# Strassen-Winograd for three weight blocks: seven half-size products in place of eight in layer 0's in-projection

## The reference

```python
for l in range(2):
    h = rms_norm(x, norm_mix[l])
    x = x + mixer_l(h)            # one input projection, two kinds of heads, one output projection
    h = rms_norm(x, norm_ffn[l])
    x = x + hierarchical_moe(h)   # 32 experts, top-1 group, top-2 inside it
```

```python
rq, rk, rv, rg, hq, hf, hi, hg = split(h @ w_in, 8)
ret = rms_norm(retention(rope(rq), rope(rk), rv)) * silu(rg)
o   = rms_norm(hgrn2(silu(hq), 1 - f(hf), hi, log f(hf))) * silu(hg)
return concat([ret, o]) @ w_out
```

## Time and profile before

| | us |
|---|---|
| median of 3 runs | 1168.29 (1167.1 to 1169.87) |
| the profiled execution | 1165.02 |
| its span in the trace | 1163.2 |
| TensorE busy in the span | 883.9 (76%) |
| VectorE busy in the span | 221.5 (19%) |
| ScalarE busy in the span | 130.3 (11%) |
| DMA read | 445.61 MB from HBM |

### The profile page before, as it was taken

How to read it: one execution, slowest core, us unless ns; L and a number is a source line. 1 busy time by engine, 2 the same in 40 slices (tenths; PEclk the granted TensorE clock), 3 DMA queues, 4 the chain that set the end, 5 groups by cost and what they waited for, 6 DMA issues and landing times.

```text
span 1163.2 us, 11675 instructions
## 1 busy us (share of the span) xinstructions
PE 883.9 (76%) x5180; PEld 404.4 (35%) x5180; DVE 221.5 (19%) x478; ACT 130.3 (11%) x271; POOL 0.5 (0%) x5
## 2 busy tenths in 40 slices
PE   9999999947474747475899999996474747474768
PEld 7555545412121212121346655443131313131313
DVE  2732332100000000000127541411010101010101
ACT  3411311000000000000021431200000000000000
POOL 0000000000000000000000000000000000000000
PEclk9999999968787878787999999998787878787889
DMA  9776769999999999999996577799999999999996
GB/s 348 303 297 274 280 221 374 434 433 433 433 438 433 436 433 433 431 431 416 425 422 286 181 292 294 306 438 433 433 438 435 432 433 429 433 431 433 421 425 284
DMA packets 20215, 447.49 MB, mean 385 GB/s; under 512 B 2624, under 2 KB 2880, under 8 KB 5824
## 3 DMA queue, kind: packets, MB, share of 16 engines
q1 hardware_dynamic: 20160, 446.67, 91.3%
HBM read 445.61 MB, written 1.05 MB: 384 GB/s over the span
## 4 chain that ended last, share of the span: by engine, by line
DMA 51%; PE 45%; DVE 1%; another core or an unknown queue 1%; issue 1%; ACT 1%; SPq 0%; DVEq 0%
DMA places<-in_together 43%; PE psum L692 16%; PE psum L1100 11%; PE psum L1212 5%; DMA places<-in_singles 4%; DMA places<-in_quarters 4%; PE psum L1097 4%; PE psum L610 1%; PE psum L1113 1%; PE psum L1141 1%; PE psum L593 1%; PE psum L586 0%; DMA places<-in_w_in 0%; PE psum L757 0%
## 5 line engine op out<-in xcount | busy, mean ns | idle before, releaser
L692 PE MATMUL psum<-places,mixed 128*32 128x512 f32 x3040 | 420.0, 703 | 266.5 <-DMA places<-in_together 239.3
L692 PEld LDWEIGHTS psum<-places,mixed 128*32 128x32 f32 x3040 | 110.0, 127 | 553.6 <-issue 445.1
L1100 PE MATMUL psum<-places 128*128 128x512 f32 x288 | 126.3, 593 | 0.0
L1100 PEld LDWEIGHTS psum<-places 128*128 128x128 f32 x288 | 53.6, 190 | 61.4 <-issue 61.2
L610 PEld LDWEIGHTS psum<-sel,x 128*128 128x128 f32 x528 | 60.8, 192 | 16.6 <-issue 16.0
L610 PE MATMUL psum<-sel,x 128*128 128x128 f32 x528 | 64.6, 279 | 0.3
L593 PE MATMUL psum<-y_sb,spread 128*128 128x512 f32 x128 | 59.6, 606 | 2.1 <-ACT y_sb L844 1.4
L892 DVE SCALAR_TENSOR_TENSOR sig<-psum,slot_scale,sig 128x512 f32<-128x512 f32 x16 | 12.0, 750 | 238.3 <-ACT sig L835 238.3
L895 DVE SCALAR_TENSOR_TENSOR mixed<-psum,slot_scale,sig 128x512 f32<-128x512 f32 x16 | 12.0, 751 | 230.0 <-PE psum L692 230.0
L905 DVE COPY y_sb<-psum 128x512 f32<-128x512 f32 x14 | 9.7, 691 | 192.4 <-PE psum L692 192.4
L837 ACT COPY mixed<-psum 128x512 f32<-128x512 f32 x16 | 9.4, 586 | 323.7 <-PE psum L617 323.7
(11 more groups left out here) (259 smaller groups left out, 524.8 us busy)
## 6 DMA issues: line engine op xcount, KB each, us to landing
places<-in_singles SPq DMA_DIRECT2D x28, 2048.0 KB, 11.6
places<-in_quarters SPq DMA_DIRECT2D x22, 2048.0 KB, 35.8
places<-in_w_in SPq DMA_DIRECT2D x12, 2048.0 KB, 26.7
places<-in_w_out SPq DMA_DIRECT2D x4, 2048.0 KB, 14.0
places<-in_singles SPq DMA_DIRECT2D x4, 1024.0 KB, 5.2
places<-in_quarters SPq DMA_DIRECT2D x4, 1024.0 KB, 46.5
places<-in_singles SPq DMA_DIRECT2D x2, 1280.0 KB, 6.1
places<-in_w_in SPq DMA_DIRECT2D x2, 1024.0 KB, 26.8
```

Of the source, the lines that this page charges most:

```text
L692: mm = pe.matmul(psum[slots, out + n, :], inp[:, c, slots], slot(layer, unit)[:, at + 512 * n:at + 512 * (n + 1)], start=c == 0, stop=c == ...
L1100: mm = pe.matmul(banks[:, m, :], hT[:, c, m * P:(m + 1) * P], w[:, c, :], start=c == 0, stop=c == KC - 1)
```

## The change

For units 5, 6 and 7 (`SEVEN`), the 256x1024 by 1024x512 product is cut in two along each dimension: A into A11, A12, A21, A22 (token half, width half; each 128x512), B into B11, B12, B21, B22 (each 512x256), the result into four corners c11, c12, c21, c22 of 128x256. `project_seven` computes seven products of such blocks, each by 4 matmuls of 128x128 by 128x256, instead of the eight that the plain product has. VectorE makes the sums of blocks (`sides_of_seven` once, `first_sums`, `second_sum` and the last line of `add_fourth_product` for each unit, in part in place in the weights) and joins the products (`keep_first_product` to `add_corner`). The four side blocks and two weight sums lie in place 9, so the DMA of expert unit 9 moves in SP's order from behind `roped` 2 to behind unit 1. VectorE's order is rewritten, with `gated_norm` cut into `norm_asked`, `refine_root`, `norm_out` and `norm_gained` among the joins; ScalarE's waits for these units are for `summed` (5 for each unit) in place of the unit's end.

```diff
+SEVEN = (5, 6, 7)
...
-                    sp.wait_ge(S["roped"], 2)
-                    load_expert_unit(0, 9)
                     load_expert_unit(0, 3)
...
                     load_expert_unit(0, 1)
+                    load_expert_unit(0, 9)
                     sp.wait_ge(S["gated"], 2)
...
+            def project_seven(n, meanwhile=()):
+                k = SEVEN.index(n)
...
+                def product(dst, left, right, opens):
+                    for c in range(4):
+                        mm = pe.matmul(dst, left[:, c, :], right[:, c, :], start=opens and c == 0, stop=c == 3,
+                                       skip_group_check=True)
+                    return mm
+                product(c11, hT[:, 0:4, 0:P], w[:, 0:4, 0:256], True).then_inc(S["product"], 1)
+                pe.wait_ge(S["sums_ready"], 2 * k + 1)
+                product(c22, side_2, sum_b, True).then_inc(S["product"], 1)
+                pe.wait_ge(S["summed"], 5 * k + 1)
+                product(c12, side_1, sum_a, False).then_inc(S["product"], 1)
+                pe.wait_ge(S["summed"], 5 * k + 2)
+                product(c21, side_3, w[:, 0:4, 256:512], False).then_inc(S["product"], 1)
+                for step in meanwhile:
+                    step()
+                pe.wait_ge(S["summed"], 5 * k + 3)
+                product(c11, hT[:, 4:8, 0:P], w[:, 4:8, 0:256], False)
+                product(c12, side_4, w[:, 4:8, 256:512], False).then_inc(S["product"], 1)
+                pe.wait_ge(S["summed"], 5 * k + 4)
+                pe.wait_ge(S["sums_ready"], 2 * k + 2)
+                product(c21, hT[:, 4:8, P:SEQ], w[:, 0:4, 0:256], False).then_inc(S["unit_used"], 1)
...
-            project(0, 5)
+            project_seven(5)
...
-            project(0, 6)
+            project_seven(6)
...
-            project(0, 7, {8: (lambda: turn_half(0, 0),)})
+            project_seven(7, (lambda: turn_half(0, 0),))
...
+            def sides_of_seven():
+                a11, a12, a21, a22 = hT[:, 0:4, 0:P], hT[:, 4:8, 0:P], hT[:, 0:4, P:SEQ], hT[:, 4:8, P:SEQ]
+                turn(V.tensor_tensor(side_1, a21, a22, ALU.add))
+                turn(V.tensor_tensor(side_2, side_1, a11, ALU.subtract))
+                turn(V.tensor_tensor(side_3, a11, a21, ALU.subtract))
+                turn(V.tensor_tensor(side_4, a12, side_2, ALU.subtract))
...
+            def first_sums(k):
+                b11, b12, b21, b22 = blocks_of(k)
+                wait_unit(dve, 0, SEVEN[k])
+                if k > 0:
+                    dve.wait_ge(S["product"], 5 * k - 2)
+                turn(V.tensor_tensor(sum_a, b12, b11, ALU.subtract))
+                turn(V.tensor_tensor(sum_b, b22, sum_a, ALU.subtract))
+            def second_sum(k):
+                b11, b12, b21, b22 = blocks_of(k)
+                V.tensor_tensor(b12, b22, b12, ALU.subtract).then_inc(S["sums_ready"], 1)
+            def keep_first_product(k):
+                dve.wait_ge(S["product"], 5 * k + 1)
+                and_wait(dve, V.tensor_copy(corner, corners(SEVEN[k])[0]), S["summed"], 5 * k + 1)
...
+            def add_fourth_product(k):
+                c11, c12, c21, c22 = corners(SEVEN[k])
+                b11, b12, b21, b22 = blocks_of(k)
+                dve.wait_ge(S["product"], 5 * k + 4)
+                V.tensor_tensor(c22, with_c12, c21, ALU.add).then_inc(S["summed"], 1)
+                V.tensor_tensor(b11, b21, sum_b, ALU.subtract).then_inc(S["sums_ready"], 1)
+            def add_corner(k):
+                c11, c12, c21, c22 = corners(SEVEN[k])
+                dve.wait_ge(S["product"], 5 * k + 5)
+                V.tensor_tensor(c12, c12, corner, ALU.add)
+                wait_projected(dve, SEVEN[k] + 1)
+                V.tensor_tensor(c21, c21, corner, ALU.add).then_inc(S["summed"], 1)
...
             rope_ret(3, GROUP_W)
+            sides_of_seven()
+            first_sums(0)
+            second_sum(0)
             mask(1, st2[:, 1, :], const("causal_scale"))
+            keep_first_product(0)
+            add_second_product(0)
+            add_third_product(0)
+            add_fourth_product(0)
+            first_sums(1)
+            second_sum(1)
+            add_corner(0)
             mask(2, st2[:, 2, :], const("causal_scale"))
...
+            norm_asked(0)
             mask(7, st2[:, 3, :], const("causal_scale"))
+            keep_first_product(1)
+            refine_root(dve, turn)
+            add_second_product(1)
+            norm_out(0, 6, 0)
+            add_third_product(1)
+            norm_gained(0, 0)
+            add_fourth_product(1)
+            first_sums(2)
+            add_corner(1)
+            second_sum(2)
+            silu_gate(6, gates_in[0])
+            gate_it(0, gates_in[0], 0)
+            keep_first_product(2)
+            norm_asked(1)
+            add_second_product(2)
+            refine_root(dve, turn)
+            add_third_product(2)
+            norm_out(1, 4, GROUP_W)
+            add_fourth_product(2)
+            norm_gained(1, GROUP_W)
+            add_corner(2)
+            silu_gate(7, gates_in[1])
+            gate_it(1, gates_in[1], GROUP_W)
```

More of the change, by code:

```diff
@@ L207, in build @@
         sin_t, cos_t = rope[:, 0], rope[:, 1]
+        at_nine = wide[:, (9 - RING) * UNIT:(10 - RING) * UNIT]
+        sum_a, sum_b = [at_nine[:, 1024 * i:1024 * (i + 1)].rearrange("p (c n) -> p c n", c=4) for i in range(2)]
+        side_1, side_2, side_3, side_4 = [at_nine[:, 512 * i:512 * (i + 1)].rearrange("p (c t) -> p c t", c=4) for i in range(4, 8)]
         val = part(0, 10, 1024, "p (c n) -> p c n", c=TC)
@@ L233, in build @@
         spread = sb("spread", [P, TC, P])[:, :, :]
+        corner, with_c12 = flat_pair(spread), flat_pair(sel)
         sig = sb("sig", [P, FF])[:, :]
@@ L267, in build @@
         names = ["small_landed", "tables_landed", "in_half_landed", "begin_landed", "begin_second", "begin_third", "begin_fourth", "gains_landed", "xt_first_landed", "xt_second_landed", "xt_third_landed", "even_dims", "odd_dims", "gather_begun", "xT_begun", "half_landed", "x_first_landed", "x_second_landed", "first_landed", "pos_landed", "lb_landed", "router_landed", "masks0_landed", "masks_landed", "consts_landed", "filler_ready", "unit_used", "stored",
-                 "act_turn", "dve_turn", "rope_args", "rope_ready", "pos_ready",
+                 "act_turn", "dve_turn", "product", "sums_ready", "summed", "rope_args", "rope_ready", "pos_ready",
                  "squares", "x_start_turned", "hT_first", "hT_second", "diag_ready", "row_done", "f_scaled", "q_scaled", "lb_in", "lb_exp",
@@ L355, in proj, with corners @@
             return psum[:, 2 * (g % 2):2 * (g % 2) + 2, :]
+        def corners(n):
+            banks = proj(n)
+            return [banks[:, tc, 256 * h:256 * (h + 1)] for tc in range(2) for h in range(2)]
         def wait_projected(eng, n):
@@ L1104, in project @@
                 mm.then_inc(S["unit_used"], 1)
+            def project_seven(n, meanwhile=()):
+                k = SEVEN.index(n)
+                wait_unit(pe, 0, n)
+                pe.wait_ge(proj_used[n % 2], n // 2)
+                w = slot(0, n).rearrange("p (c n) -> p c n", c=KC)
+                c11, c12, c21, c22 = corners(n)
+                def product(dst, left, right, opens):
[18 more added lines that the diff above has]
+                product(c21, hT[:, 4:8, P:SEQ], w[:, 0:4, 0:256], False).then_inc(S["unit_used"], 1)
             def project_first():
@@ L1475, in keep_values @@
             def keep_values(dst, g, ready):
-                wait_projected(act, g + 1)
+                if g in SEVEN:
+                    act.wait_ge(S["summed"], 5 * SEVEN.index(g) + 5)
+                else:
+                    wait_projected(act, g + 1)
                 scaled(flat(dst), g, ACT.Copy).then_inc(S["val_ready"], 1)
@@ L1515, in _ @@
             take_root(act, turn)
-            wait_projected(act, 7)
+            act.wait_ge(S["summed"], 10)
             scaled(gates_in[0], 6, ACT.Sigmoid).then_inc(S["gate_sig"], 1)
@@ L1523, in _ @@
             keep_first_half(0)
-            wait_projected(act, 8)
+            act.wait_ge(S["summed"], 15)
             scaled(gates_in[1], 7, ACT.Sigmoid).then_inc(S["gate_sig"], 1)
@@ L1884, in silu_gate @@
                 and_wait(dve, r, proj_used[g % 2], 4)
[L1886 to L1895, removed]
             def gate_it(which, gate, col):
@@ new lines, in blocks_of @@
+            def blocks_of(k):
+                w = slot(0, SEVEN[k]).rearrange("p (c n) -> p c n", c=KC)
+                return w[:, 0:4, 0:256], w[:, 0:4, 256:512], w[:, 4:8, 0:256], w[:, 4:8, 256:512]
+            def first_sums(k):
[5 more added lines that the diff above has]
+                turn(V.tensor_tensor(sum_b, b22, sum_a, ALU.subtract))
@@ new lines, in second_sum, with add_second_product @@
+            def second_sum(k):
[4 more added lines that the diff above has]
```

(29 more changed lines are left out.)

## The result

| | kernel before | changed kernel |
|---|---|---|
| median, us (runs) | 1166.53 (6) | 1160.77 (6; 1160.28 to 1162.42) |
| ratio, 95% interval | | 0.9948 [0.9934, 0.9963] |
| profiled execution, us (span) | 1165.02 (1163.2) | 1162.42 (1160.6) |
| VectorE busy, us | 221.5 | 245.7 |
| records of TensorE | 5180 | 5252 |

The change is faster by 5.8 us between these medians (4.3 to 7.7 by the interval). The forecast was 4.9 us, and as a time 1163.4 with 1161.0 to 1167.2 around it. The measured 1160.77 lies 2.6 us under that time and 0.2 us under that range.

A forecast was written before the change was run, and what follows sets the result against it. TensorE was taken to bound units 5 to the out-projection, ahead of DMA-bound experts; -4.95 us on TensorE and +0 to 0.3 at `mask(2)` gave -4.9, so 1168.3 became 1163.4 us, range 1161.0 to 1167.2.

The forecast's parts named there:

- The bound: Unit 5 to out-projection: TensorE all the way; time saved there starts the expert load stream earlier, pass-through 1.
- The products: Units 5 to 7: seven products take 12.08 us a block against 13.73, saving 4.95 us over three.
- The first two rivals: Waits bare weight loads, 2.9 us lost (with small join stalls 0.11); 256-column matmuls bound by loads, slower, up to 1195 (0.04).
- The third: Rival: the gain isn't passed on, the expert loads begin no earlier, 1168.3, no change; chance 0.07.
- VectorE's work: Sums and joins for units 5 to 7 add 25 to 28 us on VectorE, covered by TensorE's other work.
- The tightest place: End of unit 5 at `mask(2)`: mask 0.3 us ahead or level, so up to 0.3 us may be lost.
- The moved load: Unit 9's 2 MB load behind unit 1 fits idle DMA time: costs nothing, up to 4.7 us if running at 172.7.
- as a median 1168.3 - 4.9 = 1163.4 us: Whole kernel: the 4.9 us gain subtracted from the median of the runs shown, 3.3 us above the profiled execution's 1165.02.
- the sum: Whole kernel: -4.95 us on TensorE, +0 to 0.3 at `mask(2)`, 0 elsewhere: -4.9 us.
- Theory 1: From the follow-ups: only TensorE's seven products count, 4.9 us; the rest of 5.8 is partly differing sets of before runs.

The follow-up runs named there:

- eleven: Changed kernel with each unit's first product computed five times, so eleven products in a block: 1182.43 us, ratio 1.0128 to the kernel before.
- halves: Kernel before with each 512-column matmul of units 5 to 7 cut into two of 256: 1166.88 us, ratio 1.0002.
- eighth: Changed kernel with each unit's first product computed twice, so eight products, all else kept: 1166.21 us, ratio 0.9998 to the kernel before.
- sums_twice: Changed kernel with VectorE computing unit 6's two first weight sums twice: 1164.54 us, ratio 0.997 to the kernel before.
- moved_load: Kernel before with only expert unit 9's DMA moved behind unit 1 in SP's order: 1167.03 us, ratio 1.0003.
- late_nine: Changed kernel with expert unit 9's load moved to the end of the loads ahead of the expert stream: 1162.27 us, ratio 0.9964 to before.
- moved_halves: Kernel before with both unit 9's load moved behind unit 1 and units 5 to 7 in 256-column matmuls: 1165.75 us, ratio 0.9994.
- sum_a_twice: Changed kernel with only the first weight sum of unit 6 computed twice: 1161.63 us, ratio 0.9953 to the kernel before.
- no_cover: Changed kernel with TensorE's waits for joins 1 to 3 one product earlier: 1168.32 us, ratio 1.0005 to the kernel before.
- sums_twice_busy: Changed kernel with unit 6's two first sums computed twice and four filler matmuls ahead of scores_ret(1): 1161.91 us, ratio 0.9951 to before.

## Why the prediction held in its mechanism and missed in its number

**The bound.** Right, but for one reading: the chain is not TensorE all the way. Between units 5 and 6 it has one mask of VectorE, 0.57 us at 102.29 before and at 100.89 after, which the change leaves as it was. TensorE sets the rest of this stretch: the time taken from it moves the start of the expert loads one for one (4.69 and 4.70 us), and eleven shows the same for time added, up to the end of the program, within its interval.

**The products.** Right: 4.93 us in the trace for 4.95. Both halves of the argument were tested alone: matmuls of 256 columns cost what unit 1's did (halves), and with eight products nothing is gained (eighth). The first two rivals are gone by the same runs. The third, a gain that isn't passed on, is gone as a whole; what it has of truth is in the last paragraph of this section.

**VectorE's work.** 24.2 us more were measured, 25 to 28 predicted; I had added each sum at its full record, and operations that don't wait for each other begin some 0.1 us before the last has ended (95.37 behind 95.04 + 0.42 in the rows above). All of it was covered. The tightest place was the right one, with 0.67 us of room where I had 0 to 0.3, so nothing was lost there. What I had not priced is what lies behind that edge: in the profiled execution of sums_twice the granted clock fell behind the wait of 1.61 us, and the price there was double.

**The moved load.** Right: nothing (moved_load), with room to spare (at the worst place it could be put, late_nine, it cost some 1.1 us, if anything).

**The step that failed: "as a median 1168.3 - 4.9 = 1163.4 us".** The subtraction started from the median of three runs as if it were fixed. The runs of the kernel before scatter (1163.25 to 1170.3 over all lists, standard deviation 1.6 us), so a median of three is itself uncertain by about 1 us. All later medians of it lie at 1166.45 to 1166.87; from there the sum gives 1161.5 to 1162.0, inside the range. Of the 2.6 us between forecast and result the base is 1.8 (1168.29 against 1166.53 for all six runs of the same set). The profiled execution, 1165.02, had stood 3.3 us under the three, and I noted it without drawing the consequence for the lower end: 1161.0 left 2.4 us below the forecast for an uncertain base and uncertain sizes together. Nor does 1161.0 follow from its own words: "1.5 us for the scatter of the runs below" the forecast's 1161.8 would be 1160.3, and the result would have been in. That the base was high is luck of three runs; that the range had no place for it is the mistake.

**A second part, the size, stays open.** Three sets of runs gave 5.8, 5.6 and 5.9 us by their medians and 6.1, 5.3 and 5.7 by their ratios, the sum 4.9. Each interval holds 4.9, but all three lie above it. Taken together (17 runs of the changed kernel against 52 of before, means of each set compared, an estimate) they give 5.8 with a standard error of 0.3, so that chance alone is a poor account of the rest. Theory 1 had the whole of it as the base; that explains the time, and not this rest of 0.4 to 1.2 us. Moved load and 256 columns together may hold a part (eighth and moved_halves both lean that way, and neither edit alone does), but no run shows it. The traces point the other way. The prediction's sum, set against the profiled execution, was 1160.1; it took 1162.42, only 2.6 us under the 1165.02 of before. More broadly, the profiled executions of the changed kernel (1162.42, 1161.13, 1160.32) have a mean of 1161.3, those of before, moved_load, halves and moved_halves (1165.02, 1165.57, 1165.79, 1166.35) one of 1165.7, 4.4 us apart, with about 0.1 us of that from the halved matmuls. So 4.9 lies between what the traced executions and the timed ones say. Which of the two is nearer was not settled.

**Pass-through scatters by about 1 us inside layer 0's stream.** Before, a chain row has 30.21 us for the second large load. In the changed kernel, in sum_a_twice and in eighth it is, in this order (first rows of three chains):

```profile
205.06 31.26 DMA places<-in_together
```

```profile
205.35 31.18 DMA places<-in_together
```

```profile
208.60 30.10 DMA places<-in_together
```

From the start of the out-projection to the load of the last quarters (issued at 542.20 in before, 538.79 in the changed kernel) it is 405.76 us before, and 405.6 to 406.0 in moved_load, halves, moved_halves, eighth, no_cover and sums_twice_busy. It is 407.0, 406.4 and 406.9 in the three traces of the changed kernel, 406.9 in sum_a_twice and 407.3 in late_nine: there 0.7 to 1.5 us were given back in that stretch. An early start is not the reason, or not the only one, for sums_twice and eleven, whose out-projections began at 134.96 and 151.95, took 406.7 and 406.9 as well. What the load runs into was not found, and behind it the traces scatter by more (619.7 to 623.2 us from there to the end), so that it can't be followed to the total.

## What to carry to other kernels

Fewer multiplications by sums of blocks pay where TensorE sets the end, another engine is idle, and every join has a product of TensorE ahead of it: the same arithmetic with the waits one product earlier gave all of it back (no_cover). Price a late hand-over not only by the wait, but by where the granted clock goes behind it. And before a forecast of half a per cent is turned into a time, ask how well the starting median is known; the sign and the rough size were within reach, the absolute number was not.

## What the hardware showed that was not expected

Each of these comes from one profiled execution. After 1.61 us without a matmul, in a stretch otherwise dense, the granted clock fell to 0.50 for the next 3 us or so, and pairs of records of 128 columns went from 0.22 to 0.43 us (sums_twice). Waits of about 0.6 us, three in a row with a product of 2 us between (no_cover), and one of 0.35 us (sum_a_twice), left it at 1.00. A product of eight records that begins after such a wait takes 0.28 us longer than one in an unbroken stream, nearly all of it in the first record (no_cover).
